# A state space kernel's first weight tile multiplied in plain fp32 as its pieces land

## The reference, cut to what matters

```python
def s5_mixer(x, w_in, lam_re, lam_im, log_dt, b_re, b_im, c_re, c_im, d_skip, w_glu, b_glu, w_out):
    u, z = jnp.split(x @ w_in, 2, axis=-1)            # w_in: 2048 x 2048, the product of this case
    dt = jnp.exp(log_dt)[:, None]
    mag = jnp.exp(lr * dt)
    ar, ai = mag * jnp.cos(li * dt), mag * jnp.sin(li * dt)
    ...
    bbar_r = cr[..., None] * br - ci[..., None] * bi  # the first rotation
    bbar_i = cr[..., None] * bi + ci[..., None] * br
    ...                                               # scan over positions, h_r and h_i
    y = einsum(c_re, h_r) - einsum(c_im, h_i) + d_skip * u
    g = jax.nn.gelu(y)
    y = g * jax.nn.sigmoid(g @ w_glu + b_glu)
    return (y * jax.nn.silu(z)) @ w_out
```

## Time and profile before

| | us |
|---|---|
| median of 3 runs | 3073.32 (3072.61 to 3074.46) |
| the profiled execution | 3077.65 |
| its span, first to last instruction | 3075.9 |
| TensorE busy | 2987.6 (97%) |
| VectorE busy | 2135.0 (69%) |
| ScalarE busy | 1698.8 (55%) |

### The profile page before, as it was taken

How to read it: one execution, slowest core, us unless ns; L and a number is a source line. 1 busy time by engine, 2 the same in 40 slices (tenths; PEclk the granted TensorE clock), 3 DMA queues, 4 the chain that set the end, 5 groups by cost and what they waited for, 6 DMA issues and landing times.

```text
span 3075.9 us, 60005 instructions
## 1 busy us (share of the span) xinstructions
PE 2987.6 (97%) x23663; PEld 2473.3 (80%) x23730; DVE 2135.0 (69%) x3048; ACT 1698.8 (55%) x2246; POOL 40.9 (1%) x39
## 2 busy tenths in 40 slices
PE   8899999999999899999999899999999999999998
PEld 7878999999998799988998787777767777777654
DVE  7976444555657775756599997777777777777655
ACT  6644344666645433744444684445656656566676
POOL 1000000000000210000000000000000000000000
PEclk9899999999999999999999999999999999999999
DMA  6255565444473433536655426655566666656564
GB/s 229 70 202 202 171 190 173 150 144 147 135 266 100 136 116 111 177 107 195 207 172 178 131 83 207 200 191 197 193 197 187 199 197 192 201 189 202 197 200 151
DMA packets 143960, 529.87 MB, mean 172 GB/s; under 512 B 16992, under 2 KB 17760, under 8 KB 142048
## 3 DMA queue, kind: packets, MB, share of 16 engines
q1 hardware_dynamic: 141120, 515.57, 51.9%
q10 hardware_dynamic: 2592, 10.68, 1.0%
HBM read 521.99 MB, written 4.19 MB: 171 GB/s over the span
## 4 chain that ended last, share of the span: by engine, by line
PE 79%; DVE 15%; ACT 2%; DMA 2%; issue 2%; DVEq 0%; SPq 0%; ACTq 0%
PE ps L299 28%; PE ps L2844 22%; PE ps L2773 17%; DVE mem L271 4%; DMA mem<-weights 2%; DVE mem L3150 2%; PE ps L440 1%; DVE mem L3153 1%; PE ps L911 1%; PE ps L1311 1%; PE ps L1933 1%; PE ps L1343 1%; PE ps L1919 1%; DVE mem L2619 1%; DVE mem L2620 1%
## 5 line engine op out<-in xcount | busy, mean ns | idle before, releaser
L271 DVE TENSOR_TENSOR mem<-mem,rounded 128x1024 bf16<-128x1024 f32 x940 | 1142.8, 1226 | 690.5 <-ACT rounded L264 677.5
L264 ACT CAST rounded<-mem 128x1024 fp32r<-128x1024 f32 x940 | 979.1, 1046 | 902.2 <-PE ps L299 276.8
L299 PE MATMUL ps<-rounded 128*128 128x256 f32 x3168 | 447.2, 290 | 19.1 <-DVE mem L271 19.1
L299 PE MATMUL ps<-rounded,mem 128*128 128x256 bf16 x3168 | 417.0, 276 | 0.9 <-DVE mem L2573 0.5
L299 PEld LDWEIGHTS ps<-rounded 128*128 128x128 f32 x3168 | 397.2, 191 | 23.3 <-issue 17.9
L299 PE MATMUL ps<-mem,rounded 128*128 128x256 bf16 x3168 | 401.1, 273 | 2.2 <-DVE mem L271 2.2
L299 PEld LDWEIGHTS ps<-rounded,mem 128*128 128x128 bf16 x3168 | 297.1, 97 | 57.3 <-issue 1.9
L2844 PE MATMUL ps<-rounded 128*128 128x512 f32 x1024 | 335.9, 442 | 2.1 <-DVE mem L3197 2.1
L299 PEld LDWEIGHTS ps<-mem,rounded 128*128 128x128 bf16 x3168 | 300.7, 98 | 44.0 <-issue 1.9
L3179 DVE TENSOR_TENSOR mem<-mem,ps 128x512 f32<-128x512 f32 x392 | 268.3, 684 | 52.1 <-PE ps L2844 43.4
L2934 ACT CAST mem<-mem 128x1024 bf16<-128x1024 f32 x204 | 213.4, 1046 | 160.1 <-DMA mem<-experts 73.3
(11 more groups left out here) (442 smaller groups left out, 2736.4 us busy)
## 6 DMA issues: line engine op xcount, KB each, us to landing
mem<-experts SPq DMA_DIRECT2D x512, 512.0 KB, 4.1
mem<-weights SPq DMA_DIRECT2D x440, 512.0 KB, 3.7
mem<-x_t SPq DMA_DIRECT2D x4, 512.0 KB, 10.1
mem<-x_rows SPq DMA_DIRECT2D x1, 2048.0 KB, 11.7
mem<-cmp_w_k ACTq DMA_DIRECT2D x4, 512.0 KB, 4.9
mem<-cmp_w_v ACTq DMA_DIRECT2D x4, 512.0 KB, 6.0
h_rows<-mem SPq DMA_DIRECT2D x1, 2048.0 KB, 9.9
mem<-h_rows ACTq DMA_DIRECT2D x1, 2048.0 KB, 7.6
```

Of the source, the lines that this page charges most:

```text
L264: self.nc.scalar.copy(self.parts(r % SLOTS)[0], self.raw(r % RAW)).then_inc(self.high_done, with_skipped(c))
L271: self.nc.vector.tensor_tensor(wl, self.raw(r % RAW), wh.bitcast(F32), ALU.subtract).then_inc(self.low_done, with_skipped(c))
L299: mm = self.nc.tensor.matmul(self.ps[:, bank, half * 256:half * 256 + 256], a, b, start=(part == 0 and n == 0), stop=(part == PIECES - 1 a ...
```

## The change

One constant, PLAIN = 1, takes tile 0 out of the ring, as FIRST_TILES are. Its four pieces are fetched to a place of their own (the memory that later holds u and z), each behind the x part that it goes with. TensorE multiplies it in plain fp32 from the x and the weights that landed: 8 products of 256 columns for a piece, 32 for the tile, each piece when its own two transfers are in. Neither halves of pieces 0 to 3 are made. `low_done` and `high_done` are raised by four at the start by two small fills on VectorE, so that counting goes on as before. The two C matrices are issued by SyncE behind the last piece of tile 0, and no longer by ScalarE; ring pieces 4 to 6 follow them without a wait. ScalarE casts x part 0, makes the exponential and sines, casts x parts 1 to 3, then pieces 4 to 7, and only then packs B; in the loop over tiles it casts nothing beside tile 0. VectorE begins with the arithmetic on the parameters and makes the four low parts of x behind it. The rest of the diff puts `ring(c)` where places of a later piece were counted by c itself.

```diff
+PLAIN = 1
+WHOLE_TILES = (*range(PLAIN), *FIRST_TILES)
...
 def ring(c):
 
-    return c - PIECES * sum(c >= PIECES * (t + 1) for t in FIRST_TILES)
+    return c - PIECES * sum(c >= PIECES * (t + 1) for t in WHOLE_TILES)
 
 
 def place_before(c):
 
     before = c - SLOTS
-    return before - PIECES * sum(before < PIECES * (t + 1) <= c for t in FIRST_TILES)
+    return before - PIECES * sum(before < PIECES * (t + 1) <= c for t in WHOLE_TILES)
...
-        if c >= SLOTS:
+        if r >= SLOTS:
             act.wait_ge(self.multiplied, m * per + (place_before(c) + 1))
         self.nc.scalar.copy(self.parts(r % SLOTS)[0], self.raw(r % RAW)).then_inc(self.high_done, with_skipped(c))
 
...
-    loaded, consts, bc_in, skip_in = (k.sem(n) for n in "s5_params consts_landed s5_matrices s5_channels".split())
+    plain_in = [k.sem(f"plain_pieces_landed_{n}") for n in range(PLAIN * PIECES)]
+    plain = [k.at(o, 4096) for o in (S5_UZ, S5_COS)]
+    loaded, consts, b_in, c_in, skip_in = (k.sem(n) for n in
+                                           "s5_params consts_landed s5_b s5_c s5_channels".split())
...
         for n in range(PIECES):
             sp.dma_start(x_raw[:, n * 1024:(n + 1) * 1024],
                          ins["x_t"][:, n * 1024:(n + 1) * 1024]).then_inc(x_in[n], 16)
-            if n < RAW:
-                sp.dma_start(k.raw(n), ins["weights"][n]).then_inc(k.landed[n], 16)
-                k.issued += 1
+            sp.dma_start(plain[0][:, n * PIECE:(n + 1) * PIECE], ins["weights"][n]).then_inc(plain_in[n], 16)
+        for o, name in ((0, "s5_c_re"), (1024, "s5_c_im")):
+            sp.dma_start(ct[0][:, o:o + 1024], ins[name]).then_inc(c_in, 16)
+        for n in range(PIECES, PLAIN * PIECES):
+            at_ = (n - PIECES) * PIECE
+            sp.dma_start(plain[1][:, at_:at_ + PIECE], ins["weights"][n]).then_inc(plain_in[n], 16)
+        k.issued = PLAIN * PIECES
         k.stream(sp, AT_GLU, ahead=2 * RAW)
         sp.wait_ge(h_ready, 4)
         sp.dma_start(rows, ins["x_rows"]).then_inc(xs, 16)
...
         a = k.stepper(act, k.astep)
         act.dma_start(par, ins["s5_states"]).then_inc(loaded, 16)
         for o, name in ((0, "s5_b_re"), (1024, "s5_b_im")):
-            act.dma_start(b2[:, o:o + 1024], ins[name]).then_inc(bc_in, 16)
+            act.dma_start(b2[:, o:o + 1024], ins[name]).then_inc(b_in, 16)
         act.dma_start(k.at(-WORK0, 256), ins["consts"]).then_inc(consts, 16)
-        for o, name in ((0, "s5_c_re"), (1024, "s5_c_im")):
-            act.dma_start(ct[0][:, o:o + 1024], ins[name]).then_inc(bc_in, 16)
         act.dma_start(small[:, 0:16], ins["s5_channels"]).then_inc(skip_in, 16)
         act.wait_ge(loaded, 16)
         nc.scalar.activation(q["dt"], q["ldt"], ACT.Exp).then_inc(dt_ready, 1)
-        for n in range(2):
-            high(act, n)
-            k.high(act, n)
+        high(act, 0)
         act.wait_ge(angle, 1)
         a(nc.scalar.activation(q["mag"], q["lrdt"], ACT.Exp))
         a(nc.scalar.activation(q["s"], q["r"], ACT.Sin))
         a(nc.scalar.activation(q["sh"], q["half"], ACT.Sin), trig)
-        for n in range(2, PIECES):
+        for n in range(1, PIECES):
             high(act, n)
-            k.high(act, n)
+        for c in range(PLAIN * PIECES, (PLAIN + 1) * PIECES):
+            k.high(act, c)
+
...
-        act.wait_ge(bc_in, 64)
+        act.wait_ge(b_in, 32)
         make_dense(dense[1], b2, b_in_dense)
+        act.wait_ge(c_in, 32)
         a(nc.scalar.mul(ct[0][:, 1024:], ct[0][:, 1024:], -1.0), negated)
...
         for t in range(N_A_IN):
             for c in range(PIECES):
-                if t + 1 < N_A_IN:
+                if PLAIN <= t < N_A_IN - 1:
                     k.high(act, PIECES * (t + 1) + c)
                 if c == 1:
                     beside(t)
...
-                            a, b = channel_products(k.parts(piece % SLOTS), parts,
+                            a, b = channel_products(k.parts(ring(piece) % SLOTS), parts,
                                                     slice(kk * 512 + sub * P, kk * 512 + sub * P + P),
...
-        k.multiply(pe, AT_A_IN, 4, xT, "channel", ready=x_low)
+        for t in range(PLAIN):
+            pe.wait_ge(k.bank_free, t + 1)
+            for part in range(PIECES):
+                pe.wait_ge(x_in[part], 16)
+                pe.wait_ge(plain_in[PIECES * t + part], 16)
+                for kk, half_ in itertools.product(range(KC // PIECES), range(2)):
+                    w_at, kc = part * PIECE + kk * 256 + half_ * P, part * (KC // PIECES) + kk
+                    mm = nc.tensor.matmul(ps[:, t, half_ * 256:half_ * 256 + 256], plain[t][:, w_at:w_at + P],
+                                          x_raw[:, kc * T:(kc + 1) * T], start=(part == 0 and kk == 0 and half_ == 0),
+                                          stop=(part == PIECES - 1 and kk == KC // PIECES - 1 and half_ == 1),
+                                          skip_group_check=True)
+                mm.then_inc(k.multiplied, 1)
+        k.multiply(pe, AT_A_IN + PLAIN, 4 - PLAIN, xT, "channel", ready=x_low)
...
         del v.n[id(k.bank_free)]
+        nc.vector.memset(k.spare[:, 4:5], 0.0).then_inc(k.low_done, PLAIN * PIECES)
+        nc.vector.memset(k.spare[:, 5:6], 0.0).then_inc(k.high_done, PLAIN * PIECES)
         tt, ts_, stt = nc.vector.tensor_tensor, nc.vector.tensor_scalar, nc.vector.scalar_tensor_tensor
-        pieces = iter(range(PIECES * AT_A_IN, PIECES * (AT_A_IN + N_A_IN)))
+        pieces = iter(range(PIECES * (AT_A_IN + PLAIN), PIECES * (AT_A_IN + N_A_IN)))
...
-        x_low_of(0)
-        low(1)
         dve.wait_ge(dt_ready, 1)
         v(tt(q["lrdt"], q["lr"], q["dt"], ALU.mult))
         v(tt(q["x"], q["li"], q["dt"], ALU.mult))
@@ -991,9 +1011,8 @@
         v(tt(q["t1"], q["li"], q["li"], ALU.mult))
         v(tt(q["inv"], q["inv"], q["t1"], ALU.add))
         v(nc.vector.reciprocal(q["inv"], q["inv"]))
-        for n in range(1, PIECES):
+        for n in range(PIECES):
             x_low_of(n)
-            low(1)
         dve.wait_ge(trig, 1)
...
-            sp.dma_start(k.raw(c % RAW), src).then_inc(k.landed[c % RAW], 16)
...
-            nc.scalar.copy(v_tops[c % SLOTS], k.raw(c % RAW))
+            nc.scalar.copy(v_tops[ring(c) % SLOTS], k.raw(ring(c) % RAW))
```

More of the change, by code:

```diff
@@ L908, in gated_pieces @@
                             out = ps[:, t % BANKS + 3 * sub, :]
-                            a, b = token_products(k.parts(piece % SLOTS), parts, slice(kk * 512, (kk + 1) * 512),
+                            a, b = token_products(k.parts(ring(piece) % SLOTS), parts, slice(kk * 512, (kk + 1) * 512),
                                                   slice(c * T + sub * P, c * T + sub * P + P))[i]
@@ L944, in tensor @@
                     c = part * (ECH // PIECES) + kk
-                    a, b = token_products(k.parts(piece % SLOTS), yy_parts, slice(kk * 512, (kk + 1) * 512),
+                    a, b = token_products(k.parts(ring(piece) % SLOTS), yy_parts, slice(kk * 512, (kk + 1) * 512),
                                           slice(c * T + sub * P, c * T + sub * P + P))[i]
@@ L2721, in load @@
                    else k.ins["experts"][at_])
-            sp.dma_start(k.raw(c % RAW), src).then_inc(k.landed[c % RAW], 16)
+            sp.dma_start(k.raw(ring(c) % RAW), src).then_inc(k.landed[ring(c) % RAW], 16)
         def step(j, m, looped):
@@ L2767, in up_piece @@
                 kc = part * (KC // PIECES) + kk
-                a, b = channel_products(k.parts(c % SLOTS), hT,
+                a, b = channel_products(k.parts(ring(c) % SLOTS), hT,
                                         slice(kk * 256 + half * P, kk * 256 + half * P + P),
@@ L2838, in down @@
                     for i, half in itertools.product((0, 1, 2) if tt == 0 else (2, 1, 0), range(2)):
-                        a, b = token_products(k.parts(c % SLOTS), gparts[j % 2],
+                        a, b = token_products(k.parts(ring(c) % SLOTS), gparts[j % 2],
                                               slice(half * BANK, (half + 1) * BANK),
@@ L2842, in down @@
                         if i == 2 and dense(j, m):
-                            b = v_tops[c % SLOTS][:, half * BANK:(half + 1) * BANK]
+                            b = v_tops[ring(c) % SLOTS][:, half * BANK:(half + 1) * BANK]
                         mm = nc.tensor.matmul(ps[:, bank, :], a, b,
@@ L2931, in top @@
             act.wait_ge(g_low, BODY * (UNROLLED - 1) + 4)
-            act.wait_ge(k.landed[c % RAW], (m * (PER // RAW) + (ring(c) // RAW + 1)) * 16)
+            act.wait_ge(k.landed[ring(c) % RAW], (m * (PER // RAW) + (ring(c) // RAW + 1)) * 16)
             act.wait_ge(k.multiplied, m * PER + (c - SLOTS + 1))
-            nc.scalar.copy(v_tops[c % SLOTS], k.raw(c % RAW))
+            nc.scalar.copy(v_tops[ring(c) % SLOTS], k.raw(ring(c) % RAW))
         def step(j, m, looped):
```

## The result

The changed kernel took 3079.86 us (median of 20 runs, 3075.76 to 3085.28), the kernel before on the same chips 3076.33 us (20 runs, 3072.42 to 3078.27). The ratio is 1.0012 with a 95% interval of 1.0006 to 1.0017: some 3.5 us **slower**, where 1.4 us were forecast, and outside the forecast's range of 3069.7 to 3078.5. The verdict "no difference" (within 0.2%) holds; the size and the place of the loss do not. About 3.0 us of the distance to the forecast 3074.7 lie in its base, since the first three runs of before (median 3073.32) were at the low end of the 20: with the base of all 20 the same sum gives 3077.7, and the same range ends at 3081.5. The rest, 2.1 us, is the subject here. The profiled execution has a span of 3080.1 us against 3075.9. One execution of all that follow, 5069 us at a granted clock of 0.55 in after_slot176, is left out of every ratio and mean.

A forecast was written before the change was run, and what follows sets the result against it. TensorE, busy for 97% of the span, was taken as the bound, with the first stage deciding any shift. Median 3073.32 us plus 0.2 (rotation start) and 1.2 (low clock) gave 3074.7 us, no difference; range 3069.7 to 3078.5.

The forecast's parts named there:

- The new gate: First stage: VectorE's rotation waits for B's packing, now behind piece 7's cast; about 3.3 us of waiting, 27.7 to 31.0.
- the anchor: Start of VectorE's first rotation, through which alone the first 30 us matter; 30.82 moves to 31.0, +0.2 us.
- the early gate: Rival: piece 7 does not hold up the rotation, which starts at 27.7; everything 3.1 us earlier, 3070.2 us; chance 0.12.
- Plain tile hidden behind piece 7: TensorE's first tile in plain fp32 ends at 23.7 or 25.1, covered by the wait for piece 7 until 28.3.
- The fetch of piece 7: First stage: 3.8 us from release of the ring place to landing, so piece 7 is in at 27.4.
- The prediction's other estimate: Piece 7's fetch with a fixed part of about 2.0 us: 3.3 us, rotation at 30.5.
- The clock drop: TensorE returns from its wait for piece 7 at low clock: 1.6 us, bounds 0 and 3.2, +1.2 after 0.4 room.
- reach the end whole: After the first 175 us: dense TensorE work passes any first-stage gain or loss on to the end in full.
- except for the numbers of its buffers: Stages after the first 175 us: the change alters only buffer numbers there; no time was counted for them.
- the size for the whole: Whole kernel: +0.2 us at the rotation's start and +1.2 us from the low clock, 1.4 us later.
- The base: Time of the kernel before that the sum starts from: median of the runs, 3073.32 us.

The follow-up runs named there:

- after_slot176: Changed kernel with the body of TensorE's expert loop laid at instruction 176 of its block of 256; ratio 1.0007.
- pack_first: Changed kernel with ScalarE's packing of B put ahead of its casts of pieces 4 to 7; 3077.35 us, ratio 0.9999.
- after_pad64: Changed kernel with 64 instructions that do nothing added in an idle time of TensorE, restoring later instruction numbers of the kernel before; 3077.09 us, ratio 1.0009.
- after_hint: Changed kernel with the jump back of TensorE's expert loop announced at the head of each iteration; 3072.50 us, ratio 0.9992.
- before_hint: Kernel before with the jump back of TensorE's expert loop announced at the head of each iteration; 3072.18 us, ratio 0.9985.
- before_slot152: Kernel before with only the body of TensorE's expert loop moved, to instruction 152 of its block of 256; 3085.89 us, ratio 1.0031.
- before_slot88: Kernel before with only the body of TensorE's expert loop moved, to instruction 88 of its block of 256; 3076.61 us, ratio 1.0005.
- after_slot24: Changed kernel with the body of TensorE's expert loop laid at instruction 24 of its block of 256; ratio 1.0009.
- pack_hint: Changed kernel with B packed ahead of the casts of pieces 4 to 7 and TensorE's jump back announced; 3068.52 us, ratio 0.9981.
- after_slot152: Changed kernel with the body of TensorE's expert loop laid at instruction 152 of its block of 256; 3087.11 us, ratio 1.0038.

## Why the prediction was wrong

- *The new gate, pieces 4 and 7, the packing, the anchor at +0.2 us*: right, each within 0.1 us. pack_first shows that the gate was the cause of the lost gain: without it TensorE resumes 3.1 us earlier, the forecast's own figure for the early gate.
- *Plain tile hidden behind piece 7*: right, 23.65 against 23.7.
- *The fetch of piece 7, 3.8 us from the rows*: right, 3.9 us from the end of piece 4's subtraction to the cast. The prediction's other estimate, 3.3 us, from the Trainium skill, "DMA: Bandwidth & Descriptors", section "Anatomy of one DMA — SWDGE (gpsimd) path", does not fit: the section is on transfers that GpSimd issues, and this one is issued by SyncE.
- *The clock drop, 1.6 us*: right in kind. It lasted 3.4 us in five of the nine profiled executions that have this wait and 6.8 us in four, which is the span of its bounds: the five are 0.7 to 1.0 us late at 131 us, the four 1.7 to 2.0, and the forecast was 1.4.
- *"Everything after the first 175 us is dense TensorE work, which the change does not touch except for the numbers of its buffers, so a microsecond gained or lost in the first stage should reach the end whole"*: **the step that failed**, in both halves. That it reaches the end whole: the wait at 202 us took up 1.7 of 2.0 us in one execution and nothing in that of after_pad64. The rows needed were in the trace of before, a wait of 5.46 us at 202.16; only TensorE's entry into that layer was read. That the size for the whole, 1.4 us, is still fair (1 to 2 us is what after_hint and before_hint differ by) is luck in part: the forecast had no term for this wait or for the clock behind it.
- *That the change does not touch the rest "except for the numbers of its buffers"*: the other half, and the missing term. It shortened TensorE's program ahead of a loop and so moved the loop against the block ends. By the medians (3079.8 for the changed kernel, 3073.0 with the jump announced, against some 3076 and 3071.8) the turns and the fetches in mid-body cost the changed kernel 6.8 us and the kernel before about 4: some 2.5 us of the measured 3.5. That fetches cost it this much more is measured; that it is by the loop's place rests on before_slot152, where place alone costs 9 us, and on the 1.9 us, standard error 0.7, between the changed kernel and the three with the loop elsewhere. The direct attempt the other way, before_slot88, came out too small to tell. A term of 0 was set for all this, without a row, and no rival had it.
- *The base*: 3073.32 was taken from three runs, and is 3.0 us below the median of 20. This alone is the larger part of the miss, and without it the measured 3079.86 would lie inside a range of the same width. A kernel whose executions scatter over 6 us needs that much in its range.

What stays open: how a late ring piece makes TensorE's turn dearer, step by step, and how much of the changed kernel's loss one should expect in a given execution. The 1.0009 of after_pad64 and after_slot24, with cheap turns, is no puzzle: 2.3 us above before by the means, against 1.2 to 1.8 us for the change alone, is within the noise of both.

## What to carry to other kernels

An edit ahead of a long loop moves the loop in the program, and this can cost or bring more than the edit itself: here 0.3% from the position alone. Before judging small edits to a kernel with such loops, hold the body in place or announce the jump back, so that it costs nothing anywhere; here that alone was worth 4 us, and made the worth of the change (a loss of 1 to 2 us) and of the repaired change (pack_hint, 3.0 us below before_hint by the means of 22 runs each, 2.4 when each is set against the kernel before on its chip, standard error 0.5) measurable. And take the base of a forecast from more than three runs. When a stage is said to carry the end, follow the difference through the next long wait, and don't stop at the stage's last row.

## What the runs showed of the hardware

- TensorE's jump back over some 1840 instructions: the packet with the first block starts 1.1 to 3.3 us behind the jump and the first product follows 2.6 to 3.3 us later, partly hidden by up to 3.66 us of queued products. With the jump announced 1 packet was fetched in 645 us instead of 44.
- Where such a packet of 16 KB (0.9 to 1.6 us in the kernel before, up to 2.2 in before_slot152) starts 0.4 to 1.3 us behind SyncE's turn, the half-MB ring piece issued just ahead of that turn takes 4.4 to 5.5 us instead of 3.2 to 3.4, in a stretch where DMA is busy for some 60%.
- Dear turns can bring the clock down as well: in after_slot152 the gap of 2.32 us at 2633.6 was followed by the low level (granted clock 0.57 from 2636 to 2640). The gap of 2.74 us in the changed kernel was not.
- A VectorE operation on 128x32 values took 3.59 us at 5.96, beside GpSimd's clearing of the dense matrices: it ended at 9.55, GpSimd's last fill at 9.51. Operations of this shape take 0.19 us at 24 to 25 us. It cost nothing here, since what follows it was done before piece 4, for which ScalarE waited 4.08 us.
